# Six projection pieces placed between the pieces of the modulation product

## The reference

```python
shift, scale, gate = split(silu(c) @ w_mod + b_mod, 3)       # the same for c_ctx
h  = rms_norm(x,   norm_w) * (1 + scale)   + shift
hc = rms_norm(ctx, norm_w) * (1 + scale_c) + shift_c
aq, ak, av, az, ab, aa, bq, bk, bv, bz, br = split_in(h @ w_in)   # hc @ w_in likewise
a = gated_delta_net(short_conv(aq, ak, av), ...)   # both directions, context first
b = attention(bq, bk, bv) * silu(bz)
out = x + gate * (merge(a, b, br) @ w_out)
```

## Time and profile before

| | us |
|---|---|
| median of 3 runs | 2049.53 |
| lowest and highest run | 2048.87, 2054.26 |
| span of the profiled execution | 2050.0 |
| PE busy | 1942.2 (95%) |
| DVE busy | 939.4 (46%) |
| ACT busy | 620.4 (30%) |
| POOL busy | 231.1 (11%) |

### The profile page before, as it was taken

One profiled execution on the slowest core, in us unless ns is written; L12 is line 12 of the kernel. 1 busy time (PEld: TensorE's weight loads), 2 busy tenths in 40 slices (PEclk: granted clock), 3 DMA queues, 4 the chain that ended last, 5 costly groups with the idle time before them and its releaser, 6 DMA issues.

```text
span 2050.0 us, 39188 instructions
## 1 busy us (share of the span) xinstructions
PE 1942.2 (95%) x17278; PEld 1521.1 (74%) x17278; DVE 939.4 (46%) x1823; ACT 620.4 (30%) x1057; POOL 231.1 (11%) x385
## 2 busy tenths in 40 slices
PE   5679999999999999999999999899999889999999
PEld 2138888888777777777887877778887566678887
DVE  1323343565334555445445445575435644354333
ACT  4313222223143333222332322442235333322121
POOL 0000000000022222211112211311100101110000
PEclk9999999999999999999999999999999999999999
DMA  8872121223232222222221222667633222464333
GB/s 310 297 236 62 52 62 54 60 82 87 62 93 59 60 73 67 60 64 64 73 64 53 64 64 74 201 217 228 204 113 114 82 87 85 161 213 133 118 118 103
DMA packets 159474, 229.28 MB, mean 112 GB/s; under 512 B 10352, under 2 KB 108905, under 8 KB 157897
## 3 DMA queue, kind: packets, MB, share of 16 engines
q1 hardware_dynamic: 136841, 157.14, 25.9%
q0 software_dynamic: 14688, 55.48, 8.1%
q10 hardware_dynamic: 7776, 14.16, 1.9%
HBM read 203.15 MB, written 23.59 MB: 111 GB/s over the span
## 4 chain that ended last, share of the span: by engine, by line
PE 83%; DMA 6%; ACT 5%; DVE 4%; issue 2%; POOL 1%; SPq 0%; ACTq 0%; DVEq 0%; POOLq 0%
PE psum L1390 22%; PE psum L1392 20%; PE psum L1391 20%; DMA w_raw_mod<-w_mod_dram 3%; PE psum L1668 2%; PE psum L1457 2%; PE psum L1453 2%; PE psum L1514 1%; ACT inv L671 1%; PE psum L1465 1%; DVE w_lo L898 1%; PE psum L1420 1%; PE psum L1688 1%; PE psum L1655 1%; ACT w_hi L605 1%
## 5 line engine op out<-in xcount | busy, mean ns | idle before, releaser
L898 DVE TENSOR_TENSOR w_lo<-w_raw,w_hi 128x1024 fp32r<-128x1024 f32 x232 | 290.6, 1253 | 579.5 <-ACT w_hi L605 579.1
L605 ACT ACTIVATE w_hi<-w_raw 128x1024 fp32r<-128x1024 f32 x232 | 245.4, 1058 | 991.4 <-PE psum L1392 949.6
L1390 PE MATMUL psum<-h_hi,w_hi 128*128 128x512 f32 x1152 | 482.1, 419 | 13.8 <-DVE w_lo L898 11.6
L1392 PE MATMUL psum<-h_hi,w_lo 128*128 128x512 f32 x1152 | 454.1, 394 | 0.0
L1391 PE MATMUL psum<-h_lo,w_hi 128*128 128x512 f32 x1152 | 453.1, 393 | 0.0
L1390 PEld LDWEIGHTS psum<-h_hi,w_hi 128*128 128x128 f32 x1152 | 217.7, 189 | 56.2 <-DVE w_lo L898 8.3
L1392 PEld LDWEIGHTS psum<-h_hi,w_lo 128*128 128x128 f32 x1152 | 217.2, 189 | 50.5
L1391 PEld LDWEIGHTS psum<-h_lo,w_hi 128*128 128x128 f32 x1152 | 218.5, 190 | 33.0
L968 DVE SCALAR_TENSOR_TENSOR conv_acc<-conv_in,convw,conv_acc 128x772 f32<-128x772 f32 x96 | 98.2, 1023 | 3.4
L1390 PE MATMUL psum<-w_hi,m_hi 128*128 128x512 f32 x256 | 99.6, 389 | 0.0
L1391 PE MATMUL psum<-w_lo,m_hi 128*128 128x512 f32 x256 | 99.6, 389 | 0.0
(11 more groups left out here) (307 smaller groups left out, 2907.5 us busy)
## 6 DMA issues: line engine op xcount, KB each, us to landing
w_raw<-w_in_dram SPq DMA_DIRECT2D x168, 512.0 KB, 3.8
w_raw_mod<-w_mod_dram SPq DMA_DIRECT2D x64, 512.0 KB, 5.6
w_raw_modg<-w_mod_dram POOLq DMA_DIRECT2D x32, 512.0 KB, 4.4
w_raw<-w_out_dram SPq DMA_DIRECT2D x32, 512.0 KB, 3.7
gate_scratch<-gate_stage ACTq DMA_DIRECT2D x48, 256.0 KB, 3.9
w_raw<-w_proj_a_dram SPq DMA_DIRECT2D x16, 512.0 KB, 3.9
w_raw<-w_proj_b_dram SPq DMA_DIRECT2D x16, 512.0 KB, 3.7
gates<-gate_scratch POOLq DMA_DIRECT2D x32, 256.0 KB, 4.0
```

The costliest lines, as they stand in the source:

```text
L605: act.activation(part(whi[i % 2], p), part(place, p), ACT.Copy).then_inc(S("w_hi"), 1)
L898: dve.tensor_tensor(part(wlo[i % 2], p), part(raw_of(n)[0], p), part(whi[i % 2], p).bitcast(f32), ALU.subtract).then_inc(S("w_lo"), 1)
L1390: pe.matmul(out_ap, lh, rh, start=first, stop=False, skip_group_check=shared)
L1392: return pe.matmul(out_ap, ll, rh, start=False, stop=last, skip_group_check=shared)
```

## The change

The list of pieces is reordered. Of the eight pieces of the first two conv groups, six now stand between modulation pieces: after modulation piece 23 the first quarter of group 0, after 27 that of group 1, after 36 and 42 the second quarters, after 52 and 63 (the last one) the third. The two last quarters follow, and then the list goes on as before. Since both kinds of pieces are now mixed, the buffers are counted by kind (MOD_AT for the four modulation buffers, RING_AT for the two others), also where SP waits for them. The x tiles come at every third piece, not every fourth. The last quarter's steps are moved up: its column matmuls stand inside the conv piece behind the last modulation piece, after its first k-tile. The modulation sums are moved to PSUM banks 6 and 7, since the conv groups use banks 0 to 5, and the first transposes from 7 and 6 to 0 and 1; a modulation group now waits until the columns of the one two before are read (mod_evac), not only until its rows are copied. The second conv group too waits for h_lo at each k-tile. The work that follows a conv group comes two pieces later for the second group and one later for the third (late).

```diff
+EARLY = {23: (0, 0), 27: (1, 0), 36: (0, 1), 42: (1, 1), 52: (0, 2), 63: (1, 2)}
...
-    groups, pieces = [], []
+    groups, own = [], []
 
     def group(kind, col, width, per_piece, **more):
-        g = dict(kind=kind, col=col, width=width, first=len(pieces), **more)
-        for k0 in range(0, more.get("kt", KT), per_piece):
-            pieces.append(dict(g=len(groups), kind=kind, k0=k0, nk=per_piece, col=col, width=width))
-        g["last"] = len(pieces) - 1
-        groups.append(g)
+        own.append([dict(g=len(groups), kind=kind, k0=k0, nk=per_piece, col=col, width=width)
+                    for k0 in range(0, more.get("kt", KT), per_piece)])
+        groups.append(dict(kind=kind, col=col, width=width, **more))
...
+    pieces = []
+    for i, p in enumerate(p for g in own[:8] for p in g):
+        pieces.append(p)
+        if i in EARLY:
+            group_of, quarter = EARLY[i]
+            pieces.append(own[8 + group_of][quarter])
+    pieces += [own[8 + e][3] for e in (0, 1)]
+    pieces += [p for g in own[10:] for p in g]
+    for gi, g in enumerate(groups):
+        at = [n for n, p in enumerate(pieces) if p["g"] == gi]
+        g["first"], g["last"] = at[0], at[-1]
+        g["late"] = {9: 2, 10: 1}.get(gi, 0)
+    assert len(pieces) == sum(len(g) for g in own)
...
+    mods_made = np.cumsum([p["kind"] == "mod" for p in PIECES]).tolist()
+    MOD_AT = [n for n in range(NP) if PIECES[n]["kind"] == "mod"]
+    RING_AT = [n for n in range(NP) if PIECES[n]["kind"] != "mod"]
...
-    X_AT = [1 + 4 * t for t in range(NT)]
+    X_AT = [1 + 3 * t for t in range(NT)]
     H_AT = [max(g["last"] + 2, X_AT[-1] + 5) for g in MODS if g["scale"]]
+    H_AT[-1] -= 1
+    H_PARTS_AT = [a + 1 for a in H_AT[:-1]] + [H_AT[-1]]
+    MODV_AT = [g["last"] + 2 for g in MODS[:-1]] + [MODS[-1]["last"] + 1]
...
-            if n < NM:
-                return raw_mod[n % 4], S(f"w_in_mod{n % 4}"), 16 * (n // 4 + 1)
-            return raw[n % 2], S(f"w_in{n % 2}"), 16 * ((n - NM) // 2 + 1)
+            if PIECES[n]["kind"] == "mod":
+                m = mods_made[n] - 1
+                return raw_mod[m % 4], S(f"w_in_mod{m % 4}"), 16 * (m // 4 + 1)
+            r = n - mods_made[n]
+            return raw[r % 2], S(f"w_in{r % 2}"), 16 * (r // 2 + 1)
...
-                eng.wait_ge(S("mod_rows"), gi - 1)
+                eng.wait_ge(S("mod_evac"), gi - 1)
...
-                before = n - 4 if n < NM else n - 2
-                if before >= (0 if n < NM else NM):
+                if p["kind"] == "mod":
+                    m = mods_made[n] - 1
+                    before = MOD_AT[m - 4] if m >= 4 else None
+                else:
+                    r = n - mods_made[n]
+                    before = RING_AT[r - 2] if r >= 2 else None
+                if before is not None:
...
-                        act.activation(mrow[:], bank(4 + gi % 2), ACT.Copy).then_inc(S("mod_rows"), 1)
+                        act.activation(mrow[:], bank(6 + gi % 2), ACT.Copy).then_inc(S("mod_rows"), 1)
                 for j in range(4):
-                    if n == H_AT[j] + 1:
+                    if n == H_PARTS_AT[j]:
...
-                    e = n - g["last"]
+                    e = n - g["last"] - g["late"]
...
+                for gi in range(len(MODS)):
+                    if n == MODV_AT[gi]:
...
-                    if gi == G_CONV0:
+                    if gi in (G_CONV0, G_CONV0 + 1):
...
+                        if kk == 1 and n == MODS[-1]["last"] + 1:
+                            mod_cols(mrow, 6 + (len(MODS) - 1) % 2, "mod", len(MODS))
...
-                for gi, g in enumerate(MODS):
+                for gi, g in enumerate(MODS[:-1]):
                     if n == g["last"] + 1:
-                        if gi >= 2:
-                            pe.wait_ge(S("mod_evac"), gi - 1)
                         mod_cols(mrow, 6 + gi % 2, "mod", gi + 1)
```

More of the change, by code:

```diff
@@ L135, in build @@
     MODS = [g for g in GROUPS if g["kind"] == "mod"]
-    NM = MODS[-1]["last"] + 1
     PAS = [gi for gi, g in enumerate(GROUPS) if g["kind"] == "pa"]
@@ L899, in lo_part @@
                                   ALU.subtract).then_inc(S("w_lo"), 1)
-            for b in (4, 5):
+            for b in (6, 7):
                 dve.memset(bank(b), 0.0).then_inc(S("rows_zero"), 1)
@@ L906, in _ @@
             dve.wait_ge(S("rowsT"), 2)
-            dve.tensor_copy(cols[:], bank(7, 97)).then_inc(S("cols"), 1)
-            dve.tensor_copy(convw[:], bank(6, 120)).then_inc(S("cols"), 1)
+            dve.tensor_copy(cols[:], bank(0, 97)).then_inc(S("cols"), 1)
+            dve.tensor_copy(convw[:], bank(1, 120)).then_inc(S("cols"), 1)
             def x_var(t):
@@ L1173, in _ @@
                         x_norm(t)
-                for gi, g in enumerate(MODS):
-                    if n == g["last"] + 2:
+                for gi in range(len(MODS)):
+                    if n == MODV_AT[gi]:
                         mod_columns(gi)
@@ L1344, in _ @@
             pe.wait_ge(S("rows_in"), 96)
-            pe.transpose(bank(7, 97), rows[:], ident[0:97, 0:97]).then_inc(S("rowsT"), 1)
-            pe.transpose(bank(6, 120), crows[:], ident[0:120, 0:120]).then_inc(S("rowsT"), 1)
+            pe.transpose(bank(0, 97), rows[:], ident[0:97, 0:97]).then_inc(S("rowsT"), 1)
+            pe.transpose(bank(1, 120), crows[:], ident[0:120, 0:120]).then_inc(S("rowsT"), 1)
             def x_transposes(t):
@@ L1507, in piece @@
                         return
-                    b0 = 4 + gi % 2
+                    b0 = 6 + gi % 2
                     if first and gi < 2:
```

## The result

The changed kernel takes 2063.23 us (median of 6 runs, 2060.60 to 2066.84), the kernel before in the same runs 2051.9 (2048.87 to 2058.60). The ratio is 1.0049, 95% interval 1.0031 to 1.0067: some 10 us slower. The forecast was 2051.5 with a range to 2060; I had no change as likeliest and gave slower 0.29.

What follows compares the result with a forecast made beforehand. Loads of the 64 modulation pieces were taken to bound the kernel until 138.25 us, PE afterwards. From 2049.53, -4.0 for moves and +6.6 for half clock gave 2052.1, stated as 2051.5; range 2041 to 2060.

Steps and rivals of the forecast that it cites:

- +2.6 us: Whole kernel: net change forecast, 4.0 us won by the moves at full clock against 6.6 lost to half clock.
- the ledger: Up to the second projection group's end: start, gaps and conv pieces summed to 203.0 us at full clock, against 207.1 before.
- slot 24 begins: First moved conv piece (slots number pieces in the new order): starts at 70.7 us, after the x tiles' row chain.
- gap ahead of slots 29, 46, 69: Modulation pieces before these conv pieces: four stored pieces 2.4 us; restart, weight landing and split 10.2 and 17.8 us.
- gap ahead of slots 39, 57 (h chain): Before these conv pieces, the 9.7 us chain from column matmuls to w_lo comes last: gaps 15.8 and 17.2 us.
- behind the second group: Work after the second projection group's end: later conv work was valued at 0 us.
- the clock term: Moved conv pieces behind idle PE: four half-clock stretches of 3.3 us at 1.65 each, 6.6 us.
- My bound of 8.3: Conv pieces behind five idle gaps: upper bound on half-clock loss, 5 x 1.65 us; lower bound 0.
- the start at 138.25: First conv piece of the kernel before: full clock after 2.0 us idle, taken as evidence against every gap costing.
- the slower rival: Row chain, tiles 4 and 5: slot 24 begins near 76, deciding from about 74; total 2059 us, chance 0.28.
- Edits at nothing: Banks, waits, later conv work and queue edits: value 0 us; stated bounds reach 5 us.
- the first rival: Modulation loads keep running beneath conv pieces, DMA being the bound: 2016 us; with a partial form at 2040, chance 0.25.

Runs made afterwards that it cites:

- noearly4: The changed kernel with no conv piece moved and the x tiles back at every fourth piece: 2055.40 us, ratio 0.9999 to the kernel before.
- bpad: The kernel before with 18 two-column matmuls at the start of PE's list: 2043.01 us, ratio 0.9954.
- warm: The changed kernel with 18 plain 128x512 matmuls filling PE's waits ahead of slots 24, 39, 46, 57 and 69: 2046.60 us, ratio 0.9966.
- pad: The changed kernel with 18 two-column matmuls at the start of PE's list: 2051.99 us, ratio 0.9993 to the kernel before.
- two: The changed kernel with only the first two moves, after pieces 23 and 27: 2057.10 us, ratio 1.0012 to the kernel before.
- orderh: The changed kernel, four buffers, conv pieces after 23, 32, 38, 48, 54 and 63, one on each h chain: 2066.71 us, ratio 1.0069.
- x3: The kernel before with only the x tiles moved to every third piece: 2055.41 us, ratio 1.0008.
- noearly: The changed kernel with no conv piece moved, all other edits kept except the later conv work: 2059.41 us, ratio 1.0018 to the kernel before.
- buf10h: The changed kernel with ten modulation buffers and conv pieces placed one on each h chain: 2014.05 us, ratio 0.9808 to the kernel before.
- bbuf10: The kernel before with six modulation buffers, ten from modulation piece 24 on: 2029.99 us, ratio 0.9886.
- buf10: The changed kernel with six modulation buffers, ten from modulation piece 24 on: 2036.61 us, ratio 0.9918 to the kernel before.

## Why the prediction was wrong

The mechanism was right in the main: DMA stops in a conv piece, each restart is paid for, and half clock follows the stalls. The sign was right too, but +2.6 us was less than can be told from no change, so little hung on it. What failed is the size of four terms. By the ledger's own steps, with the end of the second group forecast at 203.0 + 6.6 = 209.6 and measured at 217.7:

| Step | forecast, us | measured, us |
|---|---|---|
| slot 24 begins | 70.7 | 73.56 |
| gap ahead of slots 29, 46, 69 | 2.4, 10.2, 17.8 | 2.55, 10.27, 17.87 |
| gap ahead of slots 39, 57 (h chain) | 15.8, 17.2 | 16.73, 17.87 |
| half clock in conv pieces | 4 x 1.65 = 6.6 | 9.1, in five pieces |
| length of each of the first five pieces at full clock | 8.48 | 8.66 |
| behind the second group, the head's 1.25 us counted | 0 | -1.2 |

Down to the end of the second group the differences add up to 8.1 us. The two largest are the start of slot 24 (2.9) and the clock (2.5).

- **The step that failed is the clock term**, and next to it the start of slot 24. I took a slow stretch as 3.3 us long, one for each of four stalls, from rows in which modulation pieces ran: 6.6. All five stalls were paid for, with 9.1 us, and not at 1.65 each: slots 39 and 57, at mean clocks of 0.73 and 0.80, cost 2.8 and 1.9. In slot 39 the matmuls are slow for 6 us, from 111.64 to 117.8, not for 3.3. My bound of 8.3 was itself too low. The rule of the Trainium skill cited in the forecast (TensorE: Matmul & The Clock Gate, Part 1), as I had read it there, was the better guide than the start at 138.25 that I set against it, for all five gaps were paid for. That start was a lucky one: noearly4 and bpad ran at half clock behind the same wait of 2 us. It is this term that warm against pad prices, at 5.4 us.
- **Slot 24** begins at 73.56 us in this trace, not at 70.7, by the chain that I named as the slower rival: tiles 4 and 5 and the copies between them; tile 5's copies began 3.1 us late. It stayed below the 74 from which I let it decide, but in the traces of pad, two and orderh, which do the same up to there, it begins at 74.4, 75.3 and 76.1, past that sign and up to the rival's 76. So the rival has a part of the loss. How much of it is due to the denser tiles is not shown (x3 and noearly: 2 to 4 us, within noise).
- **h chains**: 0.9 and 0.7 us more. **Lengths**: 8.48 is from the start of one piece to the next where they run back to back; to the end of the last matmul it is 8.66, and the gaps are counted from there. **Slot 29's gap** was met by luck: the four stored pieces took 1.9 us, not 2.4, and column matmuls of 0.9 us at 83.54, which the forecast did not list, made up for it. **Edits at nothing**: nothing shows (noearly4, within 3 us); the conv work done later was not tested by itself.
- **Buffers.** That DMA stops in a conv piece and that the early pieces hide nearly nothing was right; SP's timeline shows the stop, and buf10h, against bbuf10 and orderh, that moved pieces gain once loads can run ahead of them. buf10 alone doesn't show it, for ten buffers gained as much without the change. Wrong was the ground for the first rival, that DMA bandwidth binds the kernel before: bbuf10. That rival's 2016 was met only by more buffers and another order (2014).
- **The median of before** that I argued from, 2049.53 of three runs, is 2 to 5 us under the medians of the later ones (2051.9 to 2054.6), which took the absolute number further off. So did the offset that I took as nil: in every later run whose span is known the time is 1.8 to 2.2 us above it. The change in ratio was 1.001 forecast and 1.0049 measured.

Open stays why slot 24 begins at another time from trace to trace, why some of the waits grew in the warm kernel, and what stops PE at 905.77: that the number of instructions ahead moves it is shown, what it waits for is not. Open is also how the other half of the loss divides among the later start of slot 24, the h chains and the tiles: none of these was changed by itself with a difference clear of noise.

## What to carry to other kernels

Work moved into a phase that waits for loads hides nothing if the loads' buffers are freed by the engine that the work occupies: count buffers times load time against the length of the moved work first, and try more buffers before another order. When PE idles for 2 to 4 us before each block of moved work, price a part of the block at half clock (here 1.35 to 2.8 us lost in each of five), and don't take one block that ran at full clock as proof that it is free. When a trace shows a gain or a loss of a few us, look at the same stretch in the traces of kernels that are equal up to there. And when a kernel is changed at one end, compare the traces at the far end too: two kernels that differ in the number of instructions can differ by 10 us there for no reason of the change; a control with the same number of idle instructions tells it apart.

## What the runs showed of the hardware

- Eighteen matmuls of two columns at the start of PE's list made either kernel about 10 us faster. In the traces 7 us of it lie between some 840 and 1320 us, where pauses of PE without a releaser (2.47 us at 905.77, with half clock behind it; 4.7 to 5.0 us in sum) went away.
- In 26 runs of the unchanged kernel the time goes with the mean granted clock: at 0.992 to 0.994 they took 2045.2 to 2054.7 us, at 0.981 to 0.985 2056.8 to 2066.4. That half-clock stretches which fall on the path or beside it make this spread fits the traces, but was not tested.
- Behind waits of 1.9 to 2.0 us the first conv piece of the unmoved order ran at a mean clock of 1.00 in two traces (before, x3) and of 0.50 and 0.64 in two others (noearly4, bpad).
- Three or four float32 matmuls of 128x512 in each wait ahead of a conv piece kept the clock at 1.00 in all five (warm).
- Four 0.5 MB loads in flight moved 306 GB/s, up to ten 362 GB/s.
